# A transformer block on one core: seven block products for gate and up as well, with the feed-forward in two phases

## The reference

```python
def swiglu(h, wg, wu, wd):
    return (jax.nn.silu(h @ wg) * (h @ wu)) @ wd

h = rms_norm(x, norm_ffn_g[i])
x = x + swiglu(h, ffn_w_gate[i], ffn_w_up[i], ffn_w_down[i])
```

## Time and profile before

| | |
|---|---|
| median of three runs | 2321.43 us (2320.02 to 2321.55) |
| profiled execution, its own time | 2319.32 us |
| span of its trace | 2317.5 us |
| TensorE busy (matmul row) | 2291.8 us, 99% of the span |
| VectorE, ScalarE, GpSimd busy | 1304.8, 777.8, 76.2 us |

### The profile page before, as it was taken

One profiled execution on the slowest core, in us unless ns is written; L12 is line 12 of the kernel. 1 busy time (PEld: TensorE's weight loads), 2 busy tenths in 40 slices (PEclk: granted clock), 3 DMA queues, 4 the chain that ended last, 5 costly groups with the idle time before them and its releaser, 6 DMA issues.

```text
span 2317.5 us, 30952 instructions
## 1 busy us (share of the span) xinstructions
PE 2291.8 (99%) x11963; PEld 1968.9 (85%) x11963; DVE 1304.8 (56%) x1993; ACT 777.8 (34%) x1163; POOL 76.2 (3%) x89
## 2 busy tenths in 40 slices
PE   8999999999999999999999999999999999999998
PEld 7898988889889999888888888888888888888886
DVE  5333466565665556456554646565565646464647
ACT  4332344443453434322222223223322223232322
POOL 1000000000010000000000000000000000000000
PEclk9999999999999999999999999999999999999999
DMA  5343211222123113255353544535443535253444
GB/s 162 114 118 88 77 52 49 64 61 67 53 67 128 64 65 101 88 167 146 95 152 99 152 121 118 146 109 146 118 136 109 146 96 152 90 153 119 127 109 136
DMA packets 225456, 252.81 MB, mean 109 GB/s; under 512 B 14172, under 2 KB 188273, under 8 KB 224161
## 3 DMA queue, kind: packets, MB, share of 16 engines
q1 hardware_dynamic: 218050, 222.36, 30.2%
q0 software_dynamic: 7264, 28.51, 6.4%
HBM read 223.55 MB, written 4.19 MB: 98 GB/s over the span
## 4 chain that ended last, share of the span: by engine, by line
PE 96%; DVE 2%; ACT 1%; issue 0%; DMA 0%; POOL 0%; SPq 0%; ACTq 0%; DVEq 0%
PE ps L1261 93%; PE ps L1569 2%; DVE wl L759 1%; ACT wh L455 0%; DVE x_rows L773 0%; PE ps L1559 0%; PE ps L1605 0%; DVE x_rows L1182 0%; DVE hTl L759 0%; DVE down L1157 0%; DMA down<-in_ffn_w_down_dram 0%; DVE pbuf L1043 0%; PE ps L1308 0%; ACT x_rows L455 0%; ACT hTh L455 0%
## 5 line engine op out<-in xcount | busy, mean ns | idle before, releaser
L1261 PE MATMUL ps<-hTh,wh 128*128 128x512 f32 (+1 forms) x1968 | 763.5, 388 | 2.4 <-DVE wl L759 1.8
L1261 PE MATMUL ps<-hTh,wl 128*128 128x512 f32 (+1 forms) x1968 | 759.6, 386 | 0.0
L1261 PE MATMUL ps<-hTl,wh 128*128 128x512 f32 (+1 forms) x1968 | 759.2, 386 | 0.0
L759 DVE TENSOR_TENSOR wl<-raw,wh 128x1024 fp32r<-128x1024 f32 x298 | 363.0, 1222 | 347.4 <-ACT wh L455 345.6
L455 ACT ACTIVATE wh<-raw 128x1024 fp32r<-128x1024 f32 x298 | 314.3, 1059 | 534.5 <-PE ps L1261 420.3
L1261 PEld LDWEIGHTS ps<-hTh,wh 128*128 128x128 f32 x1968 | 369.8, 188 | 75.5 <-issue 2.2
L1261 PEld LDWEIGHTS ps<-hTh,wl 128*128 128x128 f32 x1968 | 369.6, 188 | 75.0
L1261 PEld LDWEIGHTS ps<-hTl,wh 128*128 128x128 f32 x1968 | 369.9, 188 | 72.3
L759 DVE TENSOR_TENSOR wl<-down,wh 128x1024 fp32r<-128x1024 f32 x132 | 161.3, 1222 | 157.0 <-ACT wh L455 157.0
L1261 PE MATMUL ps<-wh,opsh 128*128 128x512 f32 x616 | 240.8, 391 | 6.1 <-DVE x_rows L1182 4.3
L1261 PE MATMUL ps<-wl,opsh 128*128 128x512 f32 x616 | 240.2, 390 | 0.0
(11 more groups left out here) (181 smaller groups left out, 2019.3 us busy)
## 6 DMA issues: line engine op xcount, KB each, us to landing
raw<-in_ffn_w_gate_dram SPq DMA_DIRECT2D x176, 256.0 KB, 3.0
raw<-in_ffn_w_up_dram SPq DMA_DIRECT2D x176, 256.0 KB, 3.0
down<-in_ffn_w_down_dram SPq DMA_DIRECT2D x176, 256.0 KB, 3.2
raw<-in_nsa_w_in_dram SPq DMA_DIRECT2D x164, 256.0 KB, 3.0
raw<-in_nsa_w_out_dram SPq DMA_DIRECT2D x64, 256.0 KB, 3.0
t<-in_ffn_w_down_dram SPq DMA_DIRECT2D x44, 256.0 KB, 3.3
down<-down POOLq DMA_DIRECT2D x22, 512.0 KB, 6.0
t<-down POOLq DMA_DIRECT2D x22, 512.0 KB, 6.1
```

Of the source, the lines that this page charges most:

```text
L759: nc.vector.tensor_tensor(dst, src, hi.bitcast(f32), ALU.subtract).then_inc(done, 1)
L1261: return nc.tensor.matmul(out_, a, b, start=start, stop=stop, skip_group_check=True)
```

## The change

The feed-forward is written anew, in two phases of turns. What is ahead of it stays, except that the residual is transposed unscaled (the norm's gain is applied in ScalarE's copy out of PSUM, the row factor later).

- Phase one has 11 turns (`t < DOWN0`), one for a slab. Gate and up of a slab are the two column blocks of one product, the two halves of each 512-row group of the weights the two row blocks, and it is made of seven block products j = 0 to 6, each of four units: 28 units (positions 0 to 27) of 12 matmuls. The seven left operands (`left_hi`, `left_lo`) are formed once. The right operands of j = 0, 4 and 6 are weight blocks as loaded; those of j = 1, 2, 3, 5 are sums of blocks. `sum_a` (j = 1), `sum_b` (j = 2) and `sum_d` (j = 5) are done by VectorE, the one of j = 3 by GpSimd (`tc_done`), each on 128x1024 numbers for each unit, and each adds one more block to the sum before it.
- Products gather in three pairs of PSUM banks; ScalarE copies intermediate states out (`q1_at`, `s5_at`, `s7_at`, `s56_at`), VectorE combines them. The gate and m of turn t-1 are made at the head of turn t; 16 transposes on TensorE (`m_tiles`, before positions 4 and 8) turn m round, ScalarE copies it out, VectorE makes its sums (`m_combine`, after positions 8 and 12), and seven blocks for each slab go to a scratch tensor in memory.
- Phase two has 8 turns: four chunks of 3, 3, 3 and 2 slabs, each with two halves of the output columns, seven products of 3 (or 2) units. The products of a chunk's slabs gather in PSUM, so that the output is touched once in a turn. The left operands of a chunk are read back and split (128x512 each, one by ScalarE and one by VectorE, 77 in all) at one position each: 21 positions from position 26 of turn 10, from 15 of turns 12 and 14, and 14 positions from 15 of turn 16 (`FORM`).
- The rings `wh` and `wl` have three slots (`RING3`). The residual is written to memory before phase one and read back after it, since its place is used.

```diff
-G_UNITS, QUAD, DOWN = 16, 7, 14
-TURN = G_UNITS + DOWN
...
+CHUNKS = [(0, 3), (3, 6), (6, 9), (9, SLABS)]
+DOWN0 = SLABS
+TURNS = DOWN0 + 2 * len(CHUNKS)
+PRODUCTS = 7
+RING3 = 3
...
# GpSimd
-            for turn in range(2 * SLABS):
-                pool.wait_ge(down_loaded[0], 32 * (turn + 1))
-                pool.wait_ge(down_loaded[1], 32 * (turn + 1))
-                pool.dma_start(down[:, 1, :], down[:, 0, :], accum_op=ALU.add).then_inc(t1_summed, 16)
...
+            for t in range(TURNS):
+                U, sums = units_of(t), units_before(t)
+                for u in range(U):
+                    pool.wait_ge(tb_done, sums + u + 1)
+                    pool.wait_ge(lo_ready, unit_at(t, 2, u) + 1)
+                    pool.tensor_tensor(g1[u][:, :], g1[u][:, :], g0[u][:, :], ALU.add).then_inc(tc_done, 1)
...
# ScalarE, the high half of unit u of product j
+            def high(t, j, u):
...
+                elif j == 1:
+                    act.wait_ge(ta_done, sums)
+                elif j == 2:
+                    act.wait_ge(tb_done, sums)
+                elif j == 3:
+                    act.wait_ge(tc_done, sums)
+                elif j == 4:
+                    act.wait_ge(loaded0[u], 64 * t + 64)
+                elif j == 5:
+                    act.wait_ge(td_done, sums)
...
+                act.wait_ge(units_used, n - RING3 + 1 if n >= F0 + RING3 else (F0 - 1, F0, F0 - 3)[slot])
...
+                copy(wh[:, slot, :], src).then_inc(hi_ready, 1)
...
# VectorE
+            def low(t, j, u):
...
+                dve.wait_ge(hi_ready, n + 1)
+                lo(wl[:, slot, :], src, wh[:, slot, :], lo_ready)
...
+            for t in range(TURNS):
...
+                w_at, c22_at, y22_at, v_at, y11_at = (20, 21, None, 22, None) if up else (16, 17, 18, 19, 20) if U == 3 \
+                    else (11, 11, 12, 12, 13)
+                for pos in range(PRODUCTS * U):
+                    j, u = pos // U, pos % U
+                    if j == 1:
+                        sum_a(t, u)
+                    if j == 2:
+                        sum_b(t, u)
+                    if j == 5:
+                        sum_d(t, u)
+                    if t or pos >= RING3:
+                        low(t, j, u)
...
+                    if carry and pos == 1:
+                        products(t - 1, 1)
+                    if carry and pos == 2:
+                        c12(t - 1)
+                    if carry and pos == 3:
+                        products(t - 1, 0)
+                    if carry and pos == 8:
+                        m_combine(t - 1, 0)
+                    if carry and pos == 12:
+                        m_combine(t - 1, 1)
...
# TensorE
+                    hi, low = (left_hi[j], left_lo[j]) if up else (down_hi[j], down_lo[j])
...
+                    for tt in range(2):
+                        ts = slice(tt * P, (tt + 1) * P)
+                        for i in range(2):
+                            at = slice(i * 512, (i + 1) * 512)
+                            last = mm3(bank(2 * into + tt), (hi[:, u, i, ts], low[:, u, i, ts]), (wh[:, slot, at], wl[:, slot, at]),
+                                       j < 3 and u == 0 and i == 0, i == 1)
+                    last.then_inc(units_used, 1)
```

More of the change, by code:

```diff
@@ L331, in _ @@
                 unit(B0 + c, k_halves(B0 + c, w_out_v[3][:, :, c * 256:(c + 1) * 256], 4))
[L333 to L359, removed]
-                        continue
[L361 to L375, removed]
@@ new lines, in _ @@
+            for c in range(4):
+                for n in (B0 + 2 * c + RING, B0 + 2 * c + 1 + RING):
+                    if n < F0:
+                        split(n)
+                if c:
+                    left_evacuate(c - 1)
+                    left_high(c - 1, LEFT_LO[:3])
+                squares(c)
+                if c:
+                    act.wait_ge(left_sums, c)
+                    left_high(c - 1, LEFT_LO[3:])
+            high(0, 0, 0)
+            high(0, 0, 1)
+            left_evacuate(3)
@@ L1116, in _, with y_at @@
+            def y_at(t, half, b):
+                col = (t - DOWN0) % 2 * 1024 + b * 512
+                return x2[:, 2 * half:2 * half + 2, col:col + 512]
             for c in range(4):
@@ L1247, in _ @@
-            slab(UPS, MIXED[:RING], F0, 0, 0)
-            with dve.Fori(0, PAIRS) as i:
-                own.enter(i, 16)
-                for h in range(2):
-                    slab(MIXED, MIXED[:RING], F0 + G_UNITS + h * TURN, 1 + h, i)
-                own.leave(PAIRS)
-            slab(MIXED, MIXED[:RING], F0 + G_UNITS + (SLABS - 3) * TURN, SLABS - 2, 0)
-            slab(MIXED, DOWNS[:RING], F0 + G_UNITS + (SLABS - 2) * TURN, SLABS - 1, 0)
-            slab(DOWNS, [], F0 + G_UNITS + (SLABS - 1) * TURN, SLABS, 0)
+            nc.vector.tensor_scalar(rr[:, :], rr[:, :], 1.0 / D, EPS, ALU.mult, ALU.add).then_inc(r2_den, 1)
@@ new lines, in c21, with c12 @@
+            def c21(t):
+                dve.wait_ge(units_used, unit_end(t, 5))
+                dve.wait_ge(v_done, t + 1)
+                w = works(t)
+                nc.vector.tensor_tensor(w[1][:, :, :], w[1][:, :, :], pair(pairs_of(t)[2]), ALU.add).then_inc(c21_done, 1)
+            def c12(t):
+                dve.wait_ge(units_used, unit_end(t, 6))
+                w = works(t)
+                dst = w[0] if t < DOWN0 else w[3]
+                nc.vector.tensor_tensor(dst[:, :, :], pair(pairs_of(t)[1]), w[0][:, :, :], ALU.subtract).then_inc(c12_done, 1)
@@ L1258, in _ @@
+            c21(TURNS - 1)
+            y21(TURNS - 1)
+            c12(TURNS - 1)
+            y12(TURNS - 1)
         @block.tensor
```

702 lines of the change are left out of this document (432 added, 270 removed).

## The result

The changed kernel takes 2492.97 us (median of 4 runs, 2492.27 to 2493.03), the kernel before 2321.13 (median of 4 on the same chip): ratio 1.0741, 95% interval 1.0728 to 1.0754. It is slower by 172 us; the forecast was 114, and its range ended at 2485.

The account below looks back on a forecast made before the run. TensorE's work was taken as the bound. The span without stalls, 2225.1 us, plus 148 for serial sums gave 2373, plus 60 for GpSimd's lock 2433; the execution time was forecast as 2435 us, range 2355 to 2485.

Parts of the forecast that it names:

- GpSimd's hold: Both phases: GpSimd's 2.2 us sum delays VectorE's low half by 1.1 us, 55 times, 60 us.
- the serial sums: Both phases: sum between copy and low half takes 3.47 us against TensorE's 2.72; 82 + 66 = 148 us, formed operands included.
- all but the sums: Span without stalls: 925.4 before the kernels part, 1276.8 TensorE work, 13 start, 4 middle, 5.9 end; 2225.1 us.
- TensorE's work: Feed-forward: 5544 matmuls at 0.2265 us plus transposes, 1276.8 us, 100.3 less; a phase-one turn 77.9 us without stalls.
- Rival (c): GpSimd's sum takes 3.5 to 4.5 us, costing 55 x 2.4 to 3.4 us: 2509 to 2564 us; chance 0.12.
- The step from turn 10 to 11: Between the phases: SP waits for TensorE's last unit before a load, and 2 MB of residual return; 4 us.
- The clock: Stalls up to 3 us, as at position 9, may drop TensorE to 1.2 GHz; following positions would stall anyway, nothing added.
- (b): Both phases: serial sums alone cost time, GpSimd's sum short or not in VectorE's way; 2377 us, chance 0.26.
- (d): At positions with sums the feed keeps pace and TensorE runs on; at best 2229 us, chance 0.11.

Follow-up runs that it names:

- all four on 1 column: Changed kernel with VectorE's three sums and GpSimd's sum each cut to one column of 1024, second low half reading an unsummed copy: 2250.8 us, ratio 0.9699.
- GpSimd's on 1 column: Changed kernel with only GpSimd's sum cut to one column of 1024; waits, order and other instructions stay: 2403.5 us, ratio 1.0355.
- a, b and d ahead: Changed kernel with VectorE's sum_a, sum_b and sum_d issued one position earlier, GpSimd keeping its sum, everything computed: 2327.9 us, ratio 1.0024.

## Why the prediction was right in direction and short in size

The forecast for the span was 2433; it came out at 2490.4, 57 us more. The experiments divide the stretch behind the first sum a, and with the changed kernel's own start ahead of it they add up to its span: 953.4 + 1297.4 + 152.2 + 87.4 = 2490.4. Of the 57, 27.4 are in GpSimd's hold, 25.7 in what has nothing to do with sums, 4.2 in the serial sums.

| term | forecast | measured | by |
|---|---|---|---|
| all but the sums | 2225.1 | 2250.8 (953.4 + 1297.4) | all four on 1 column |
| serial sums, with the forms | 148 | 152.2 | GpSimd's on 1 column, less that |
| GpSimd's hold | 60 | 87.4 | changed kernel, less GpSimd's on 1 column |

**TensorE's work** was right. The turn without sums is 78.2 for 77.9; the transposes cost what was reckoned.

**The serial sums** were right in mechanism. Their total, 152.2 for 148, is right in part by luck: in the eleven turns of phase one they cost 93 for 82, in phase two, where the forecast counts the formed operands with them, 59 for 66 (measured so, the 59 has only what the formed operands add beside sums; what they cost without sums is in the row above). Sum a starts of one turn stand 3.49 apart (3.47 forecast), the turn loses 8.4 us by them (7.5 forecast), 0.1 at each of six restarts of TensorE among it. That GpSimd would change their price was not reckoned: it is the interaction of 32.5 us that sits in the row of the hold.

**GpSimd's hold is the step that failed**: "it can begin only where VectorE idles, in the 1.1 us in which ScalarE copies, and then the low half has to wait for it: 2.2 - 1.1 = 1.1 lost each". The 2.2 was right (2.24 from the end of VectorE's sum, 2.37 the shortest row), and so is the price of 1.0 where it begins in that pause. But it can begin elsewhere: GpSimd came in between two instructions of VectorE that follow on each other, and there the whole 2.2 is lost. I had taken from the earlier trace rows, where it was held through three instructions, that it would always be; rows of one case were made a rule. With two whole holds of four in phase one and 13 of 22 in phase two the term is 87.4 us, which is 1.3 for each of 66 where I had 1.1 for 55: 51.5 in phase one for 36, 35.9 in phase two for 24. The 2.2 itself owes something to luck: the rate and start of the earlier trace rows make 0.12 + 2 x 0.87 = 1.85 for two operands read one after the other, and I had put 2.2. Rival (c), a longer sum, is out: its least time, 2509, is 16 us above the measured one, and the sum is not longer; what its rows show above 2.24 is time in which it was held.

**The rest** is 25.7 us short. TensorE's first unit began at 941.4, where the terms of the forecast give 934.9. Of these 6.5 us, 2.6 were lost before the two kernels part (the same 16 transposes between units of the output projection began at 893.7 here and at 891.1 before); 2.5 in a wait of TensorE for residual additions within the projection, which VectorE now makes between combinations of the left operands, where I had let it end as before; and 1.4 behind it, where TensorE waited 3.3 us for the last additions, at 932.49, and 5.6 for the left operands. The steady turns of phase one without sums are 0.3 over 77.9, 3 us in all. Some 13 us lie in phase two, where even without sums a turn of three units takes 58 to 60 us for 57.1; TensorE's waits for low halves there sum to 8.6 us in 8 times, and no run separates the rest. The step from turn 10 to 11 cost 4.1 over the turns around it, as forecast (4).

**The clock.** "I add nothing" held in the steady turn: after the gap of 4.13 TensorE's matmuls stood 0.43 apart for 2.6 us, at a granted clock of 0.50, the lower level of 1.2 GHz, but the next low half was ready at 1344.92, later than the unit at full clock would have ended. With GpSimd's sum one position later the same stretch came twice in some turns, behind gaps of 1.94 and 2.54, and these took 93.0 for 91.4. So it is covered only where what comes next is late anyway.

**Rivals.** (b), serial sums alone, is the kernel with GpSimd's sum on one column: forecast 2377, measured 2403.5. In spans 2399.0 for 2373: 25.7 and 4.2 more by the table, 3.9 less because its shared stages were shorter. (d), the feed keeps pace, is false for this order and true for the same arithmetic in another: 2261.6.

Left open: why the shared stages varied by 4 us from kernel to kernel (the same 16 transposes began at 889.8, 891.1 and 893.7 in three of the traces). Nothing here tells; the comparisons of stretches don't need it. About 3 of the 25.7 us, in the first turn and at the end, were not assigned.

## What to carry to other kernels

Before a formation (a sum ahead of a split) is given to VectorE, look where it stands: between a copy of another engine and the instruction that follows, it makes a serial chain, and an engine that is 67% busy can be late at every position. One position earlier, the same instruction costs next to nothing (the stretch with all four sums made so is 8 us over the one without sums): 172 us slower became 60 us faster than before with not one addition less. And giving a two-operand sum to GpSimd did not relieve VectorE here, where both read SBUF: in a forecast count the whole of GpSimd's duration as VectorE's, less only the pauses that VectorE has at that very moment, and keep in the range that GpSimd's sum may itself be held for as long as VectorE's work is unbroken.

## What was not expected of the hardware

- GpSimd's addition of 128x1024 float32 takes 2.24 us from the moment it has its operands to itself, and it can come in between two VectorE instructions that stand 0.33 us apart; the one behind it then shows 2.62 for 0.42. In a row of VectorE a hold looks like a longer instruction, not like idle time. GpSimd can also be the one that waits: in the kernel with a, b and d ahead one of its rows was 8.46 us, held through six VectorE instructions that had started behind it.
- A GpSimd fill of the same size (0.95 us) ran beside VectorE's two-operand instructions with no change in either.
- Four GpSimd instructions of 256 columns alternate with VectorE's, 0.42 to 0.54 us of hold for each: splitting the work spreads the price and takes it only from 2.2 to 1.9 where VectorE has no pause.
- Each restart of TensorE after a gap as short as 0.5 us cost another 0.1: the first matmul stood 0.33 from the next instead of 0.23.
